# Suffix sums of a stick-breaking attention taken over added key blocks, and the cached keys and values loaded later

## The chip, the core and the metric

The kernel runs on one core of a Trainium2 chip. The metric is the device time of one execution in microseconds; the time before is the median of three runs, 817.32 us (816.03 to 822.58). TensorE is called PE here, its weight loads PEld, VectorE is DVE, ScalarE is ACT, GpSimd is POOL, and SP is the queue that starts most loads.

## What is computed

One layer of a hybrid trunk over 544 tokens (512 of a new stream, 32 of a running one with 256 cached frames). The part that matters here is the attention of the 512 new tokens:

```python
z = einsum('bqhd,bkhd->bhqk', q, k) * DH ** -0.5
causal = k_pos[None, :] < q_pos[:, None]
log_not = where(causal, log_sigmoid(-z), 0.0)
suffix = cumsum(log_not, axis=3, reverse=True) - log_not
a = where(causal, exp(log_sigmoid(z) + suffix), 0.0)
o = einsum('bhqk,bkhd->bqhd', a, v)
```

So the score of key s for query t gets the sum of `-softplus(z)` over the keys from s to t-1: its own and all later ones before the query. Around it stand the input projection (queries, keys, values, a pooling input, gates), a pooling branch, output projections, an MLP of 4 x 1024 hidden features, a gated input embedding and norms. The running stream attends to its 256 cached frames and its own 32.

## The kernel before, in words

Everything lies features first: a tile has 128 features as partitions and tokens as columns. Matrix products are in fp32r, and each factor is split into a high part (ACT copies it to fp32r) and a low part (DVE subtracts), so that a product is three matmuls: hi x hi, hi x lo, lo x hi. A weight tile is 128x1024; SP loads it into `raw`, `split(t)` on ACT makes `w_hi` (L635) and `split(t)` on DVE `w_lo` (L1324), up to three tiles ahead of PE. A projection tile (`tile`, L984, L987, L990) is 48 matmuls of 272 columns.

The mixer stage is a loop over four pairs of heads (`pair(i)` on PE, ACT and DVE; the first and last are written out, the middle two are a hardware loop). The order of each engine's work is written out by hand, one queue per engine. On PE a pair is: tile 0, tile 1, `sums(1, i-1)`, tile 2, `outputs(1, i-1)`, `scores(0, i)`, tile 3, `v_rows`, tile 4, tile 5, `sums(0, i)`, tile 6, `outputs(0, i)`, `scores(1, i)`, tile 7. Tiles 0 to 3 give q, k, v and the pooling input, 4 to 7 the gates. A projection result has two places in PSUM in turn: tile j may start once DVE has taken tile j-2. `gate(3, i)` (L1422) takes tile 7, so tile 1 of the next pair waits for it.

The attention of a head, g = 2i + hh, runs through these steps. Keys are partitions, in four blocks b of 128; the columns of block b are the queries of the blocks b to 3, 512, 384, 256 and 128 of them, 1280 columns in all, held in one PSUM region `z_ps` and one SBUF buffer `work` at the offsets `Z_OFF`:

- `scores` (PE) writes z; `chain` (ACT, L703, L705, L707) makes log(1 + exp(-|z|)); `stick` (DVE, L1401) adds max(z, 0): the sticks, softplus(z).
- POOL zeroes the non-causal corners of the four diagonal blocks with four selects of 128x128 (`mask_diagonals`, L584).
- `stick_hi` (ACT, L712) and `stick_lo` (DVE, L1406) split the sticks into `b_hi` and `b_lo`; the second signals `slo_done`.
- `sums` (PE, L1037) waits for `slo_done` and adds to z. For key block b and each block c from b to 3 it multiplies the sticks of block c by a constant matrix: `negtri` (a triangle of -1) for c = b, `negone` (all -1) for c > b, each for the high and the low part.
- `prob` (ACT, L718) takes exp; POOL masks again; `prob_hi` (L723) and `prob_lo` (L1411) split; `outputs` (PE, L965 to L967) multiplies by the values; `head_out` (L1417) takes the result.

In a middle pair DVE does `stick(1)`, `stick_lo(1)`, `gate(3)` at the end. In the last pair the order is `stick(1)`, `gate(3)`, `mean_lo(2)` (L1428, L1429), `group_lo(0)` (L1434), `mean_lo(3)`, `group_lo(1)`, `stick_lo(1)`, while PE does after tile 7 `group(0)` to `group(3)` (the pooling groups, six matmuls of 272 columns each, by way of L965 to L967), then `sums(1, 3)`, four `pool_part`s, `outputs(1, 3)` and then the scores against the cached keys (L1143), before which it waits for `past_in`: both loads of cached keys (`ckt`) and values (`cvn`), 512 KB each. ACT issues these loads (L786, L787) after the first pair.

Of the kernel before, what the change touches and what calls it, by code (L numbers as in the profile page):

```python
# [12 lines left out]
P = 128  # L13
# [213 lines left out]
def hybrid_step_kernel(nc, w_tiles, x_t, p_t, ck_t, cv, state_t, w_grp, vecs,  # L227
                       y_t, k_t, v_t, pool_t):
    ctx = ExitStack()
    with ctx:  # L230
# [3 lines left out]
        def sem(name):  # L234
            return ctx.enter_context(nc.semaphore(name))
# [23 lines left out]
        def at(part, name, shape, dt=F32):  # L259
            t = nc.alloc_sbuf_tensor_at(name, shape, dt, offset=place[part])  # L260
            place[part] += 4 * int(np.prod(shape[1:]))
            return t
# [3 lines left out]
        gates = at(0, "gates", [P, 2 * KT, TOK])  # L266
        upad = at(1, "upad", [P, GROUPS, PADW])
        ysb = at(1, "ysb", [P, PAIRS, TOK])
        ckt = at(1, "ckt", [P, PAIRS, PAST])
        cvn = at(1, "cvn", [P, PAST // P, HEADS * DH])  # L270
        mean0 = [at(1, "mean0_hi", [P, TOK], F32R), at(1, "mean0_lo", [P, TOK], F32R)]
        qbd = at(1, "qbd", [P, PAIRS, 2 * DEC])
# [131 lines left out]
        spm_done = sem("spm_done")  # L404
        shi_done = sem("shi_done")
        slo_done = sem("slo_done")
        c_done = sem("c_done")
        prob_done = sem("prob_done")
        pm_done = sem("pm_done")
# [213 lines left out]
        def _(act):  # L623
# [85 lines left out]
            def stick_hi(hh, i):  # L709
                g = 2 * i + hh  # L710
                act.wait_ge(spm_done, g * QB + QB)
                act.activation(b_hi[:, SOF:SOF + Z_COLS], work[:, :], ACT.Copy).then_inc(shi_done, 1)  # L712

            def prob(hh, i):
                g = 2 * i + hh

                act.wait_ge(c_done, g + 1)
                act.activation(work[:, :], z_ps, ACT.Exp).then_inc(prob_done, 1)  # L718

            def prob_hi(hh, i):  # L720
                g = 2 * i + hh
                act.wait_ge(pm_done, g * QB + QB)
                act.activation(b_hi[:, SOF:SOF + Z_COLS], work[:, :], ACT.Copy).then_inc(phi_done, 1)  # L723
# [59 lines left out]
                stick_hi(1, i)  # L783

            pair(0)
            act.dma_start(ckt[:, :, :], ck_t).then_inc(past_in, 16)  # L786
            act.dma_start(cvn[:, :, :], cv).then_inc(past_in, 16)  # L787
            with act.Fori(1, PAIRS - 1) as i:
                pair(i)
            pair(PAIRS - 1)  # L790
# [2 lines left out]
            split(T_MIX + AHEAD)  # L793
            split(T_MIX + 1 + AHEAD)
            prob(1, PAIRS - 1)
            prob_hi(1, PAIRS - 1)
            split(T_MIX + 2 + AHEAD)

# [163 lines left out]
        def _(pe):  # L962
# [65 lines left out]
            def sums(hh, i):  # L1028

                g = 2 * i + hh  # L1030
                pe.wait_ge(slo_done, g + 1)
                for b in range(QB):
                    for c in range(b, QB):
                        lhs = negtri if c == b else negone
                        z = z_ps[:, Z_OFF[b] + P * (c - b):Z_OFF[b] + Z_LEN[b]]
                        for part in (b_hi, b_lo):
                            mm = pe.matmul(z, lhs[:, :], part[:, SOF + Z_OFF[c]:SOF + Z_OFF[c] + Z_LEN[c]],  # L1037
                                           start=False, stop=(c == QB - 1), skip_group_check=True)
                mm.then_inc(c_done, 1)

            def outputs(hh, i):
# [269 lines left out]
        def _(dve):  # L1311
# [8 lines left out]
            def split(t, i=0, per=0):  # L1320

                s = t % W_RING
                dve.wait_ge(whi_done, t + 1 + i * per)
                dve.tensor_tensor(w_lo[:, s, :, :].rearrange("p k c -> p (k c)"), raw[:, t % RAW_RING, :],  # L1324
                                  w_hi[:, s, :, :].rearrange("p k c -> p (k c)"), ALU.subtract).then_inc(wlo_done, 1)
# [71 lines left out]
            def stick(hh, i):  # L1397
# [3 lines left out]
                dve.scalar_tensor_tensor(out=work[:, :], in0=z_ps, scalar=0.0, in1=work[:, :],  # L1401
                                         op0=ALU.max, op1=ALU.add).then_inc(sp_done, 1)

            def stick_lo(hh, i):
                dve.wait_ge(shi_done, 2 * i + hh + 1)
                dve.tensor_tensor(b_lo[:, SOF:SOF + Z_COLS], work[:, :], b_hi[:, SOF:SOF + Z_COLS],  # L1406
                                  ALU.subtract).then_inc(slo_done, 1)

            def prob_lo(hh, i):
                dve.wait_ge(phi_done, 2 * i + hh + 1)  # L1410
# [8 lines left out]
            def gate(jj, i):  # L1419
                j = 4 + jj  # L1420
                dve.wait_ge(full, j + 1 + i * S1_PER)
                dve.tensor_tensor(halves(gates[:, 4 * i + jj, :]), pair_result(j, i), halves(rn[:, :]), ALU.mult)\  # L1422
                   .then_inc(taken, 1)
# [14 lines left out]
            def pair(i):  # L1438
                first = isinstance(i, int) and i == 0
                last = isinstance(i, int) and i == PAIRS - 1  # L1440
                q, k, v = (ev[:, n, 0:TOK] for n in range(3))
                if not first:
                    split(AHEAD + 0, i, S1_PER)

                dve.wait_ge(full, 1 + i * S1_PER)
                dve.scalar_tensor_tensor(out=halves(q), in0=pair_result(0, i), scalar=DH ** -0.5, in1=halves(rn[:, :]),
                                         op0=ALU.mult, op1=ALU.mult).then_inc(taken, 1)
                dve.wait_ge(taken, 1 + i * S1_PER)
                for h in range(2):
                    r = slice(DH * h, DH * (h + 1))  # L1450
                    dve.tensor_copy(qbd[r, i, DEC * h:DEC * (h + 1)], q[r, SEQ:TOK])
                dve.wait_ge(qkhi_done, 2 * i + 1)
                dve.tensor_tensor(b_lo[:, QOF:QOF + TOK], q, b_hi[:, QOF:QOF + TOK], ALU.subtract)\
                   .then_inc(qklo_done, 1)
                split(AHEAD + 1, i, S1_PER)
                if not first:
                    dve.wait_ge(kv_out[0], 16 * i)
                normed(1, k, i, S1_PER, pair_result(1, i)).then_inc(taken, 1)
                dve.wait_ge(taken, 2 + i * S1_PER)
                dve.tensor_copy(kst[:, i, :], k[:, SEQ:TOK])  # L1460
                dve.wait_ge(qkhi_done, 2 * i + 2)
                dve.tensor_tensor(b_lo[:, KOF:KOF + TOK], k, b_hi[:, KOF:KOF + TOK], ALU.subtract)\
                   .then_inc(qklo_done, 1)
                split(AHEAD + 2, i, S1_PER)
                if not first:
                    prob_lo(1, i - 1)
                if not first:
                    dve.wait_ge(kv_out[1], 16 * i)
                normed(2, v, i, S1_PER, pair_result(2, i)).then_inc(taken, 1)
                dve.wait_ge(taken, 3 + i * S1_PER)  # L1470
                dve.tensor_copy(vst[:, i, :], v[:, SEQ:TOK])
                if not first:
                    head_out(1, i - 1)
                    stick(0, i)
                    split(AHEAD + 3, i, S1_PER)

                dve.wait_ge(full, 4 + i * S1_PER)
                u = upad[:, i, :]
                dve.tensor_tensor(u[:, U_PROMPT:U_PROMPT + HALF], pair_result(3, i)[:, 0, :], rn[:, 0:HALF], ALU.mult)
                dve.tensor_tensor(u[:, U_PROMPT + HALF:U_STATE], pair_result(3, i)[:, 1, 0:SEQ - HALF],  # L1480
                                  rn[:, HALF:SEQ], ALU.mult)
                dve.tensor_tensor(u[:, U_SAMPLE:PADW], pair_result(3, i)[:, 1, SEQ - HALF:HALF],
                                  rn[:, SEQ:TOK], ALU.mult).then_inc(taken, 1)
                if first:
                    stick(0, i)
                    split(AHEAD + 3)
                stick_lo(0, i)
                dve.wait_ge(vhi_done, i + 1)
                dve.tensor_tensor(b_lo[:, VOF:VOF + SEQ], o_ps, b_hi[:, VOF:VOF + SEQ], ALU.subtract)\
                   .then_inc(vlo_done, 1)  # L1490
                split(AHEAD + 4, i, S1_PER)
                gate(0, i)
                split(AHEAD + 5, i, S1_PER)
                if last:

                    dve.wait_ge(mean_done, GROUPS)
                gate(1, i)
                split(AHEAD + 6, i, S1_PER)
                if last:
                    mean_lo(0)  # L1500
                    mean_lo(1)
                prob_lo(0, i)
                gate(2, i)
                head_out(0, i)
                split(AHEAD + 7, i, S1_PER)
                stick(1, i)
                if last:
                    gate(3, i)
                    mean_lo(2)
                    group_lo(0)  # L1510
                    mean_lo(3)
                    group_lo(1)
                    stick_lo(1, i)
                    for s in kv_out:
                        dve.wait_ge(s, 16 * PAIRS)
                else:
                    stick_lo(1, i)
                    gate(3, i)

# [320 lines left out]
```

## Time and profile before

| what | value |
|---|---|
| runs, median (lowest to highest) | 817.32 us (816.03 to 822.58) |
| the profiled execution's own time | 817.61 us |
| span of the profiled execution | 815.9 us |
| PE busy | 792.6 us, 97% |
| DVE busy | 473.9 us, 58% |
| ACT busy | 370.4 us, 45% |
| POOL busy | 96.0 us, 12% |
| mean granted TensorE clock | 0.99 |

The span is from the first to the last instruction of the one execution that was profiled, and 1.7 us of its own time lie around it. Times inside the profile are microseconds from the span's start. A row of a timeline is: start, length, engine, line, operation, what it writes and reads, how many, and in brackets how long the engine stood idle before it and what released it. Matmuls overlap in their pipeline, so the pace of PE is read from start to start and not from the lengths.

### The profile page before, as it was taken

To read this page: it belongs to the slowest core of one execution; us is meant where nothing else is said; L and a number is where in the kernel's file an instruction comes from. 1 tells how busy PE (TensorE), PEld (TensorE's weight loads), DVE (VectorE), ACT (ScalarE), POOL (GpSimd) and SP (SyncE) were. 2 spreads that over 40 slices of the span, in tenths; PEclk is the share of its full clock that TensorE was granted. 3 is DMA by queue.
4 is the path that set the end of the run, shared out by engine and by line. 5 is a ranking of instruction groups with operands and counts; after the bars stand their busy time and mean duration, and the time that the engine had idled before them with its cause. 6 is when DMAs were issued, how large, how long until landed. Compare 5 with 4: busy or idle time off the path is not lost.

```text
span 815.9 us, 14392 instructions
## 1 busy us (share of the span) xinstructions
PE 792.6 (97%) x6130; PEld 780.5 (96%) x6130; DVE 473.9 (58%) x555; ACT 370.4 (45%) x423; POOL 96.0 (12%) x164
## 2 busy tenths in 40 slices
PE   8999999999998999999999999999999999999993
PEld 7899999999998989999999999999999999999993
DVE  6654354354455536687873347533773367677966
ACT  7444433433485344466552136422552145555542
POOL 1041041042061000010000200010001100100000
PEclk9999999999999999999999999999999999999997
DMA  6333231231222113967564875667574855925402
GB/s 229 118 98 119 71 94 55 87 92 52 92 69 76 53 53 104 270 181 173 177 207 130 188 199 171 170 176 182 169 197 123 206 184 165 210 72 164 116 1 110
DMA packets 32954, 110.19 MB, mean 135 GB/s; under 512 B 4480, under 2 KB 4480, under 8 KB 32896
## 3 DMA queue, kind: packets, MB, share of 16 engines
q1 hardware_dynamic: 24624, 84.72, 32.0%
q0 software_dynamic: 6016, 21.04, 14.2%
q10 hardware_dynamic: 2256, 3.60, 1.2%
q8 instruction: 45, 0.74, 0.4%
q14 instruction: 13, 0.11, 0.0%
HBM read 94.33 MB, written 4.52 MB: 121 GB/s over the span
## 4 chain that ended last, share of the span: by engine, by line
PE 88%; DVE 7%; ACT 2%; issue 2%; DMA 1%; SPq 0%; DVEq 0%; ACTq 0%
PE psum L1228 23%; PE psum L984 18%; PE psum L990 18%; PE psum L987 18%; PE psum L1037 3%; PE psum L965 2%; PE psum L967 2%; PE psum L966 2%; DVE w_lo L1324 1%; DMA raw<-w_tiles 1%; ACT w_hi L635 1%; DVE work L1348 1%; DVE xt L1750 1%; PE psum L1306 1%; DVE b_lo L1668 0%
## 5 line engine op out<-in xcount | busy, mean ns | idle before, releaser
L643 ACT ACTIVATE w_hi<-raw_more 128x1024 fp32r<-128x1024 f32 x84 | 88.7, 1056 | 136.6 <-PE psum L990 102.6
L984 PE MATMUL psum<-a_hi,w_hi 128*128 128x272 f32 x640 | 135.6, 293 | 2.7 <-DVE a_lo L1338 2.4
L990 PE MATMUL psum<-a_hi,w_lo 128*128 128x272 f32 x640 | 132.8, 289 | 0.0
L987 PE MATMUL psum<-a_lo,w_hi 128*128 128x272 f32 x640 | 132.5, 289 | 0.0
L984 PE MATMUL psum<-b_hi,w_hi 128*128 128x272 f32 x640 | 132.3, 288 | 0.0
L990 PE MATMUL psum<-b_hi,w_lo 128*128 128x272 f32 x640 | 132.2, 288 | 0.0
L987 PE MATMUL psum<-b_lo,w_hi 128*128 128x272 f32 x640 | 132.1, 288 | 0.0
L1332 DVE TENSOR_TENSOR w_lo<-raw_more,w_hi 128x1024 fp32r<-128x1024 f32 x84 | 102.4, 1223 | 36.9 <-ACT w_hi L643 36.6
L1228 PE MATMUL psum<-u_hi,w_hi 128*128 128x272 f32 x560 | 115.9, 288 | 1.1 <-issue 0.9
L1228 PE MATMUL psum<-u_hi,w_lo 128*128 128x272 f32 x560 | 115.7, 288 | 0.0
L1228 PE MATMUL psum<-u_lo,w_hi 128*128 128x272 f32 x560 | 115.5, 287 | 0.0
L984 PEld LDWEIGHTS psum<-a_hi,w_hi 128*128 128x128 f32 x640 | 100.7, 189 | 5.4 <-DVE a_lo L1338 3.4
L987 PEld LDWEIGHTS psum<-a_lo,w_hi 128*128 128x128 f32 x640 | 101.0, 189 | 0.0
L987 PEld LDWEIGHTS psum<-b_lo,w_hi 128*128 128x128 f32 x640 | 100.6, 188 | 0.0
L984 PEld LDWEIGHTS psum<-b_hi,w_hi 128*128 128x128 f32 x640 | 100.5, 188 | 0.0
L990 PEld LDWEIGHTS psum<-a_hi,w_lo 128*128 128x128 f32 x640 | 100.4, 190 | 0.0
L990 PEld LDWEIGHTS psum<-b_hi,w_lo 128*128 128x128 f32 x640 | 100.1, 189 | 0.0
L1228 PEld LDWEIGHTS psum<-u_hi,w_hi 128*128 128x128 f32 x560 | 87.8, 188 | 1.6 <-issue 1.4
L1228 PEld LDWEIGHTS psum<-u_lo,w_hi 128*128 128x128 f32 x560 | 88.4, 188 | 0.0
L1228 PEld LDWEIGHTS psum<-u_hi,w_lo 128*128 128x128 f32 x560 | 87.5, 188 | 0.0
L1324 DVE TENSOR_TENSOR w_lo<-raw,w_hi 128x1024 fp32r<-128x1024 f32 x42 | 52.7, 1255 | 58.9 <-ACT w_hi L635 58.9
L1582 DVE TENSOR_TENSOR xt<-psum,xt 128x544 f32<-128x544 f32 x40 | 28.9, 723 | 89.3 <-PE psum L990 89.3
(192 smaller groups left out, 987.4 us busy)
## 6 DMA issues: line engine op xcount, KB each, us to landing
raw_more<-w_tiles SPq DMA_DIRECT2D x84, 512.0 KB, 4.3
raw<-w_tiles SPq DMA_DIRECT2D x67, 512.0 KB, 3.5
raw_more<-w_tiles POOLq DMA_DIRECT2D x16, 512.0 KB, 7.2
raw_more<-raw_more POOLq DMA_DIRECT2D x14, 512.0 KB, 8.4
xt<-x_t SPq DMA_DIRECT2D x8, 272.0 KB, 5.1
y_t<-xt SPq DMA_DIRECT2D x8, 272.0 KB, 2.1
raw<-w_tiles POOLq DMA_DIRECT2D x4, 512.0 KB, 7.9
raw_more<-raw POOLq DMA_DIRECT2D x3, 512.0 KB, 6.4
```

Of the source, the lines that this page charges most:

```text
L643: act.activation(w_hi[:, t % W_RING, :, :].rearrange("p k c -> p (k c)"), src, ACT.Copy)\
L965: pe.matmul(out, hi, rhi, start=first, stop=False, skip_group_check=True)
L966: pe.matmul(out, hi, rlo, start=False, stop=False, skip_group_check=True)
L967: return pe.matmul(out, lo, rhi, start=False, stop=last, skip_group_check=True)
L984: pe.matmul(base[:, h, :], w_hi[:, s, wk, :], cols(hi, k, h * HALF, (h + 1) * HALF), start=(opens and q == 0), stop=False, skip_group_chec ...
L987: pe.matmul(base[:, h, :], w_hi[:, s, wk, :], cols(lo, k, h * HALF, (h + 1) * HALF), start=False, stop=False, skip_group_check=True)
L990: mm = pe.matmul(base[:, h, :], w_lo[:, s, wk, :], cols(hi, k, h * HALF, (h + 1) * HALF), start=False, stop=(closes and q == len(ks) - 1), ...
L1037: mm = pe.matmul(z, lhs[:, :], part[:, SOF + Z_OFF[c]:SOF + Z_OFF[c] + Z_LEN[c]], start=False, stop=(c == QB - 1), skip_group_check=True)
L1228: mm = pe.matmul(out[:, two, :], w_part[:, t % W_RING, 2 * k + two, :], u_part[:, op, k, :], start=(OPENS[s] and k == 0 and w_part is w_hi ...
L1324: dve.tensor_tensor(w_lo[:, s, :, :].rearrange("p k c -> p (k c)"), raw[:, t % RAW_RING, :], w_hi[:, s, :, :].rearrange("p k c -> p (k c)" ...
L1332: dve.tensor_tensor(w_lo[:, t % W_RING, :, :].rearrange("p k c -> p (k c)"), src, w_hi[:, t % W_RING, :, :].rearrange("p k c -> p (k c)"), ...
L1582: dve.tensor_tensor(halves(xt[:, m, :]), slot(n), halves(xt[:, m, :]), ALU.add).then_inc(taken, 1)
```

## The change

A second way of taking the sums of later key blocks. DVE adds up the sticks of the later blocks first, three blocks of 128 columns, into `later`; ACT and DVE split `later` into `later_hi` and `later_lo` (384 columns each). `sums` then has for each key block its own sticks against `negtri`, the next block's first 128 columns against `negone`, and for the blocks 0 and 1 the added sticks against `negone` for the rest. The new buffers lie in the place of `ckt` and `cvn`, so the loads of these move behind the last `prob`. `stick_later` stands behind `split(AHEAD + 3)` for the first head of a pair, and behind `stick(1)` for the second, in the last pair behind `gate(3)`.

```diff
@@ buffers
+        later_hi = nc.alloc_sbuf_tensor_at("later_hi", [P, 3 * P], F32R, offset=place[1])
+        later_lo = nc.alloc_sbuf_tensor_at("later_lo", [P, 3 * P], F32R, offset=place[1] + 3 * P * 4)
         ckt = at(1, "ckt", [P, PAIRS, PAST])
+        later = nc.alloc_sbuf_tensor_at("later", [P, 3 * P], F32, offset=place[1])
         cvn = at(1, "cvn", [P, PAST // P, HEADS * DH])
@@ ACT, stick_hi
                 act.activation(b_hi[:, SOF:SOF + Z_COLS], work[:, :], ACT.Copy).then_inc(shi_done, 1)
+                act.wait_ge(later_done, g + 1)
+                act.activation(later_hi[:, :], later[:, :], ACT.Copy).then_inc(laterhi_done, 1)
@@ ACT, the order
             pair(0)
-            act.dma_start(ckt[:, :, :], ck_t).then_inc(past_in, 16)
-            act.dma_start(cvn[:, :, :], cv).then_inc(past_in, 16)
             with act.Fori(1, PAIRS - 1) as i:
...
             prob(1, PAIRS - 1)
+            act.dma_start(ckt[:, :, :], ck_t).then_inc(past_in, 16)
+            act.dma_start(cvn[:, :, :], cv).then_inc(past_in, 16)
             prob_hi(1, PAIRS - 1)
@@ PE, sums
+                sticks = [(b_hi[:, SOF:SOF + Z_COLS], later_hi), (b_lo[:, SOF:SOF + Z_COLS], later_lo)]
                 for b in range(QB):
-                    for c in range(b, QB):
-                        lhs = negtri if c == b else negone
-                        z = z_ps[:, Z_OFF[b] + P * (c - b):Z_OFF[b] + Z_LEN[b]]
-                        for part in (b_hi, b_lo):
-                            mm = pe.matmul(z, lhs[:, :], part[:, SOF + Z_OFF[c]:SOF + Z_OFF[c] + Z_LEN[c]],
-                                           start=False, stop=(c == QB - 1), skip_group_check=True)
+                    at_b = Z_OFF[b]
+                    for own, _ in sticks:
+                        mm = pe.matmul(z_ps[:, at_b:at_b + Z_LEN[b]], negtri[:, :], own[:, at_b:at_b + Z_LEN[b]],
+                                       start=False, stop=(b == QB - 1), skip_group_check=True)
+                    if b == QB - 1:
+                        continue
+                    nxt = Z_OFF[b + 1]
+                    for own, _ in sticks:
+                        mm = pe.matmul(z_ps[:, at_b + P:at_b + 2 * P], negone[:, :], own[:, nxt:nxt + P],
+                                       start=False, stop=(b == QB - 2), skip_group_check=True)
+                    if b < QB - 2:
+                        more = (slice(0, 2 * P), slice(2 * P, 3 * P))[b]
+                        for _, sums_of in sticks:
+                            mm = pe.matmul(z_ps[:, at_b + 2 * P:at_b + Z_LEN[b]], negone[:, :], sums_of[:, more],
+                                           start=False, stop=True, skip_group_check=True)
@@ DVE
+            def stick_later(hh, i):
+                g = 2 * i + hh
+                one, two, three = (work[:, Z_OFF[b]:Z_OFF[b] + Z_LEN[b]] for b in (1, 2, 3))
+                dve.wait_ge(spm_done, g * QB + QB)
+                dve.tensor_tensor(later[:, 2 * P:3 * P], two[:, P:2 * P], three, ALU.add).then_inc(later_part, 1)
+                dve.tensor_tensor(later[:, 0:P], one[:, P:2 * P], two[:, 0:P], ALU.add)
+                dve.wait_ge(later_part, g + 1)
+                dve.tensor_tensor(later[:, P:2 * P], one[:, 2 * P:3 * P], later[:, 2 * P:3 * P], ALU.add)\
+                   .then_inc(later_done, 1)
             def stick_lo(hh, i):
                 dve.wait_ge(shi_done, 2 * i + hh + 1)
-                dve.tensor_tensor(b_lo[:, SOF:SOF + Z_COLS], work[:, :], b_hi[:, SOF:SOF + Z_COLS],
-                                  ALU.subtract).then_inc(slo_done, 1)
+                dve.tensor_tensor(b_lo[:, SOF:SOF + Z_COLS], work[:, :], b_hi[:, SOF:SOF + Z_COLS], ALU.subtract)
+                dve.wait_ge(laterhi_done, 2 * i + hh + 1)
+                dve.tensor_tensor(later_lo[:, :], later[:, :], later_hi[:, :], ALU.subtract).then_inc(slo_done, 1)
@@ DVE, pair
                     split(AHEAD + 3, i, S1_PER)
+                    stick_later(0, i)
...
                 if first:
                     stick(0, i)
                     split(AHEAD + 3)
+                    stick_later(0, i)
                 stick_lo(0, i)
...
                 stick(1, i)
                 if last:
                     gate(3, i)
+                    stick_later(1, i)
                     mean_lo(2)
...
                 else:
+                    stick_later(1, i)
                     stick_lo(1, i)
                     gate(3, i)
```

## Rows read from the trace of the kernel before

**Rows 1.** The page's fourth part: lines on the chain that ended last.

```profile
PE psum L1228 23%; PE psum L984 18%; PE psum L990 18%; PE psum L987 18%; PE psum L1037 3%; PE psum L965 2%; PE psum L967 2%; PE psum L966 2%; DVE w_lo L1324 1%; DMA raw<-w_tiles 1%; ACT w_hi L635 1%; DVE work L1348 1%; DVE xt L1750 1%; PE psum L1306 1%; DVE b_lo L1668 0%
```

**Rows 2.** Busy time by stretch, L1037 alone: stretch, PE, PEld, clock, DMA, GB/s.

```profile
115.20:117.90 2.70, 2.70 (x20) 2.60 (x20) 1.00 0.11 42
...
266.30:269.60 3.30, 3.26 (x20) 3.10 (x20) 0.85 0.02 5
```

**Rows 3.** Timeline of PE, one call of `sums`.

```profile
146.36 0.40 PE L1037 MATMUL psum<-b_hi,negtri 128*128 128x512 f32 x1
...
147.41 0.22 PE L1037 MATMUL psum<-b_hi,negone 128*128 128x128 f32 x1
147.47 0.27 PE L1037 MATMUL psum<-b_lo,negone 128*128 128x128 f32 x1
147.58 0.39 PE L1037 MATMUL psum<-b_hi,negtri 128*128 128x384 f32 x1
147.81 0.34 PE L1037 MATMUL psum<-b_lo,negtri 128*128 128x384 f32 x1
147.98 0.28 PE L1037 MATMUL psum<-b_hi,negone 128*128 128x256 f32 x1
...
148.84 0.28 PE L1037 MATMUL psum<-b_hi,negtri 128*128 128x128 f32 x1
...
149.07 0.46 PE L984 MATMUL psum<-a_hi,w_hi 128*128 128x272 f32 x2
```

**Rows 4.** Timelines of DVE, PE and PEld where pair 2's tile 1 begins.

```profile
137.99 1.49 DVE L1406 TENSOR_TENSOR b_lo<-work,b_hi 128x1280 fp32r<-128x1280 f32 x1 [2.44 <-ACT b_hi L712]
139.40 0.72 DVE L1422 TENSOR_TENSOR gates<-psum,rn 128x544 f32 x1
...
139.86 0.41 PE L990 MATMUL psum<-a_hi,w_lo 128*128 128x272 f32 x2
...
140.23 0.30 PEld L984 LDWEIGHTS psum<-a_hi,w_hi 128*128 128x128 f32 x2 [0.18 <-issue]
```

**Rows 5.** Timeline of DVE, the copies of tile 3 in pair 2.

```profile
165.67 0.43 DVE L1479 TENSOR_TENSOR upad<-psum,rn 128x272 f32 x1
166.02 0.40 DVE L1480 TENSOR_TENSOR upad<-psum,rn 128x240 f32 x1
```

**Rows 6.** Timeline of DVE, head 0; then L1037's starts, first to last.

```profile
47.50 2.47 DVE L1406 TENSOR_TENSOR b_lo<-work,b_hi 128x1280 fp32r<-128x1280 f32 x1 [2.24 <-ACT b_hi L712]
...
L1037 PE MATMUL psum<-b_hi,negtri x32: 275/359/796, 52.7 to 269.4; 128*128 128x512 f32 x8, 128*128 128x384 f32 x8, 128*128 128x256 f32 x8, 128*128 128x128 f32 x8
```

**Rows 7.** Timelines of DVE and POOL at the last pair's end; POOL also in pair 1.

```profile
261.69 0.68 DVE L1428 TENSOR_TENSOR b_lo<-upad,b_hi 128x512 fp32r<-128x512 f32 x1
...
263.88 0.77 DVE L1434 SCALAR_TENSOR_TENSOR a_lo<-psum,vec,a_hi 128x544 fp32r<-128x544 f32 x1
264.79 1.49 DVE L1406 TENSOR_TENSOR b_lo<-work,b_hi 128x1280 fp32r<-128x1280 f32 x1
...
261.70 0.82 POOL L584 TENSOR_SCALAR_AFFINE_SELECT work<-work 128x128 f32<-128x128 f32 x1
...
261.21 0.54 POOL L584 TENSOR_SCALAR_AFFINE_SELECT work<-work 128x128 f32<-128x128 f32 x2 [15.70 <-DVE work L1401]
...
135.63 1.02 POOL L584 TENSOR_SCALAR_AFFINE_SELECT work<-work 128x128 f32<-128x128 f32 x4 [10.87 <-DVE work L1401]
```

**Rows 8.** Busy by stretch: PE, PEld, DVE, ACT, POOL, then clock, DMA, GB/s.

```profile
260.50:263.90 3.40, 1.71 (x11) 1.38 (x11) 3.40 (x8) 1.73 (x3) 1.56 (x4) 1.00 0.49 154
263.90:267.30 3.40, 3.29 (x12) 2.62 (x11) 3.02 (x5) 2.28 (x4) 0.00 (x0) 0.50 0.00 0
```

**Rows 9.** The load of the cached values; the last `prob`; the first use.

```profile
cvn<-cv ACTq DMA_DIRECT2D x1, 512.0 KB, 4.4
...
276.87 1.22 ACT L718 ACTIVATE work<-psum 128x1280 f32<-128x1280 f32 x1
...
284.03 1.95 PE L1143 MATMUL psum<-qbd,ckt 128*128 128x64 f32 x16
```

More of the change, by code:

```diff
@@ L406, in hybrid_step_kernel @@
         slo_done = sem("slo_done")
+        later_part = sem("later_part")
+        later_done = sem("later_done")
+        laterhi_done = sem("laterhi_done")
         c_done = sem("c_done")
```

## The prediction, made before the changed kernel ran

> **What bounds the kernel now.** I read the page first: PE is busy 97% of the span, the chain that ended last is PE nearly from end to end, and L1037, the suffix sums, is 3% of it [rows 1]. So PE's time in these sums counts, and any new wait of PE costs in full. Next the view of busy time by stretch for L1037 alone: one head takes 2.7 us with the full clock, and 3.3 us for the last head, where the mean granted clock was 0.85 [rows 2]. The timeline of PE then gives the pace from start to start inside one head: 20 matmuls from 146.36 to 149.07, which is 2.71 us [rows 3]. Last I looked for places where PE already leans on DVE, since the change gives DVE more to do. There are two such places: a gap of some 0.15 us at tile 1 of the pairs 1, 2 and 3 [rows 4], and the end of the last pair, where PE goes from one DVE result to the next and the clock falls [rows 8].
>
> **What is removed from PE.** Per head the column count falls from 5120 to 4096 and the matmuls from 20 to 18. Matched piece by piece, two matmuls of 384 columns go, two of 256 become 128 wide, all others stay. A 384-column one paces at 0.17 us (147.81 to 147.98). A 128-column one takes 0.06 us right behind a wider one, but the next needs 0.11 us (147.41, 147.47, 147.58), and a pair behind other 128-column ones takes 0.23 us (148.84 to 149.07), so they pace at some 0.115 us each, no faster than the 256-column ones (about 0.12 us) [rows 3]. Gain per head: 2 x 0.17 and next to nothing for the narrowing, 0.355 us with rounding; 18 matmuls in some 2.36 us. Bounds: 2 of 20 matmuls at the mean pace, 0.27 us, taken down to 0.25; and with the narrowing paid in full (2 x 0.06), 0.46. I take 0.355, for the trace shows 128-column pairs at both paces and the new order has more of the slow kind. Eight heads: -2.84 us.
>
> The Trainium skill, TensorE: Matmul & The Clock Gate, "Wait — 56ns, not 53.3ns?", says that warm matmuls follow each other at N columns / 2.4 GHz plus about 2.5 ns. By that rule a head would gain 0.43 us and eight heads 3.45 us, 0.6 more than my sum. The rows on the 128-column pairs disagree with it here, and I go by them.
>
> **What DVE and ACT get.** No row shows an addition of 128 columns, so I take it from its neighbours: 272 columns last 0.43 us and let the next start after 0.35 [rows 5]; 512 last 0.68 [rows 7]; hence 1.04 ns a column, and pace is length less 0.08. An addition of 128: 0.28 us long, paced 0.20. The subtraction of 384: 0.55 long, paced 0.47. `stick_later` is then 0.6 us of DVE, `later_lo` 0.47, and the 384-column copy about 0.5 on ACT. Bounds for `later_lo`: the 272-column row, 0.35, and the 512-column one, 0.6.
>
> *Before the sums of heads 0 to 6.* `stick_lo` of head 0 ends at 49.97 and its sums start at 52.7 [rows 6]; this is the tightest of the seven, the others have six or seven us (139.48 to 146.36 for head 3 [rows 3, 4]). `later_lo` adds 0.5 to 1 us (`stick_lo` itself stretches from 1.49 to 2.47 beside POOL's window sums). Hidden; bounds 0 and 0.
>
> *Tile 1 of the pairs 1, 2 and 3.* Here it isn't hidden. PE's last pair of tile 0 starts at 139.86, so the next would follow at 140.11; the weights of tile 1 are loaded at 140.23. That is 0.11 us after `gate(3)` ended (139.40 + 0.72), and tile 1 needs the place that this op frees. The profile books the 0.18 us as "issue", but the same gap and distance stand at pairs 1 and 3. Before `gate(3)` stands `stick_lo`, and it starts when ACT has copied the masked sticks: a chain that began with the scores of the second head [rows 4]. `stick_later` fits beside that copy: DVE had idled 2.44 us before `stick_lo`, of which the 1.28 us behind the masks are free. `later_lo` doesn't fit, for it stands between `stick_lo` and `gate(3)`: +0.47 us, three times, +1.41 us (bounds 3 x 0.35 and 3 x 0.6; nothing, if the gap has another cause). Queued behind `gate(3)` are only `split` and the next q, which PE doesn't miss.
>
> *The last pair.* DVE goes `gate(3)`, `mean_lo(2)` at 261.69, and so on to `group_lo(1)` at 263.88 and `stick_lo` at 264.79, which ends at 266.28; PE starts the last sums then, at 266.3 [rows 2, 7]. Now `stick_later` stands before `mean_lo(2)` and waits for POOL's four masks, with all of that queued behind it and PE's `group(2)`, `group(3)` and sums waiting. The masks began at 261.21. The third lasted 0.82 us beside `mean_lo(2)`; undisturbed, four take 1.02 (135.63) [rows 7]. With DVE waiting they end at 262.24, `stick_later` starts at 262.3, and with 0.6 us and a hop `mean_lo(2)` starts at 262.95: +1.26. `stick_lo` had waited 0.14 us for ACT behind `group_lo(1)` (263.88 + 0.77 to 264.79); that slack goes, so it starts 1.1 later, and `later_lo` adds 0.47 behind it: the sums start 1.53 us later. Bounds: 1.1 (shorter additions, no hop) and 2.0 (masks at 1.56 us as before).
>
> The Trainium skill, SBUF — State Buffer, "SBUF: two separate sides", says that a DVE op with two SBUF inputs and a GpSimd op that reads SBUF lock each other out for a whole instruction. The third mask beside `mean_lo(2)` agrees. With the masks as long as before, against this rule, the sum would be 0.5 us higher.
>
> *The clock.* In 260.50 to 263.90 PE was busy for 1.71 of 3.4 us, and in the 3.4 us after that the clock was 0.50 (1.2 GHz) [rows 8]; this cost the last sums 0.6 us [rows 2]. PE's gaps get longer here. For the sum I take the same 0.6 again, so no difference; bounds -0.6 and +1.7 (one further stretch of 3.4 us at half pace on the path).
>
> *Cached keys and values.* `prob` starts at 276.87, both loads are issued while it runs, by 277.6, and PE needs them at 284.03. The values took 4.4 us to land [rows 9]: 282.0, two us early. Price 0; if SP's weight tile beside it doubled the landing, +2.4. ACT waits for POOL's masks then, so the issue is hidden.
>
> **Sum.** -2.84 + 1.41 + 1.53 = +0.10 us. The profiled execution took 817.61 us itself (span 815.9 and 1.7 around it), which gives 817.7. It lies 0.3 above the median of the runs, so I forecast 817.4 us for the median.
>
> **Rivals.**
> - *The gain comes whole.* The gap at tile 1 is PE's own ("issue", as the profile books it), and DVE's additions in the tail cost nothing because PE would idle at half clock anyway. For it: the booking. Against: PE waits on named DVE results in the tail. 817.3 - 2.84 = 814.5; with tile 1 alone free, 816.0.
> - *A second cold stretch, the slower side.* PE's gaps before the last sums grow by 1.5 us in all, and behind the gaps of 260.5 to 263.9 the clock fell [rows 8]. If the gaps before `group(2)`, `group(3)` and the sums bring a second fall behind the first, the sums and the `pool_part`s behind them run at 1.2 GHz for a further 3.4 us, half of it lost: +1.7, 819.1. It decides from the point where PE stands as idle after 264 as it did before. For it: the gaps double. Against: at half pace the two groups fill more of the time, and the sums come right behind.
> - *The narrow matmuls give less*, 0.25 us a head: +0.84, 818.2.
> - *The loads land late*: PE stands before L1143, 2.4 us at a doubled landing, 819.8. Against: two us of cover.
>
> **How the numbers follow.** Cancelled out, 817.4: 0.50. Gain whole or half: 0.17. Second cold stretch: 0.18. Narrow matmuls give less: 0.10. Late loads: 0.05. The range has the bounds of the terms in it: the low end 814.8 nearly reaches the whole gain, the high end 820.6 is the sum with `later_lo` at 0.6 (+0.4), a tail of 2.0 (+0.5), the cold stretch (+1.7) and a part of what the narrow matmuls may give less. A measurement of this kernel can tell about 1%, 8 us, from no change, and every case lies inside: within 1% 0.95, faster 0.02, slower 0.03 (one run of before was 822.58, so disturbances of that size exist).
>
> **What would show it.** Right: a head's sums from start to start in 2.35 us with 18 matmuls; the gap before tile 1 at 0.6 us where it was 0.15, behind a later `gate(3)`; `stick_lo` in the last pair later by 1.1 us and the last sums by 1.5 against tile 7; no wait before L1143. Wrong: tile 1 following without a larger gap, the clock low for more than one stretch near 264, or a wait on `past_in`.

## The result, and the profile after

Twelve runs of the changed kernel have a median of 820.82 us (817.64 to 823.29), against 817.57 us (815.99 to 822.58) of the kernel before in the same series. The ratio is 1.0031, with a 95% interval of 1.0016 to 1.0046: slower by 0.3%, clear of noise and well within 1%. The forecast was 817.4 us and no change; the ratio times the 817.32 us that it started from is 819.9, inside the range, while the median itself lies 0.2 us above the range's end. The profiled execution took 817.75 us (span 816.0), 0.14 more than the one of before, where +0.10 was forecast. So the profile has about what was worked out, and the mean of many executions turns out (below) some 2 us longer than that. The rest is about both halves.

The page's first part of the changed kernel:

```profile
PE 790.5 (97%) x6114; PEld 778.6 (95%) x6114; DVE 483.8 (59%) x587; ACT 373.6 (46%) x431; POOL 93.4 (11%) x164
```

PE has 2.1 us less to do, DVE 9.9 us more. One head's sums in the timeline of PE, changed kernel (it answers to [rows 3]):

```profile
145.21 0.40 PE L1046 MATMUL psum<-b_hi,negtri 128*128 128x512 f32 x1
...
145.68 0.22 PE L1053 MATMUL psum<-b_hi,negone 128*128 128x128 f32 x1
145.74 0.27 PE L1053 MATMUL psum<-b_lo,negone 128*128 128x128 f32 x1
145.85 0.33 PE L1058 MATMUL psum<-later_hi,negone 128*128 128x256 f32 x1
...
146.67 0.28 PE L1058 MATMUL psum<-later_hi,negone 128*128 128x128 f32 x1
146.78 0.28 PE L1058 MATMUL psum<-later_lo,negone 128*128 128x128 f32 x1
146.89 0.33 PE L1046 MATMUL psum<-b_hi,negtri 128*128 128x256 f32 x1
...
147.57 0.47 PE L994 MATMUL psum<-a_hi,w_hi 128*128 128x272 f32 x2
```

145.21 to 147.57 is 2.36 us where it was 2.71, and so for the first seven heads: 0.35 us gained each. The last head went from 3.24 to 2.47 us, for in this execution the clock was back at 2.4 GHz when its sums began. The two paces of a 128-column matmul are seen again, 0.06 us behind a wider one and 0.11 in a row.

Where pair 2's tile 1 begins, timelines of DVE and PE (to [rows 4]):

```profile
136.39 1.49 DVE L1437 TENSOR_TENSOR b_lo<-work,b_hi 128x1280 fp32r<-128x1280 f32 x1 [0.61 <-ACT b_hi L720]
137.80 0.55 DVE L1439 TENSOR_TENSOR later_lo<-later,later_hi 128x384 fp32r<-128x384 f32 x1
138.27 0.72 DVE L1454 TENSOR_TENSOR gates<-psum,rn 128x544 f32 x1
...
138.26 0.41 PE L1000 MATMUL psum<-a_hi,w_lo 128*128 128x272 f32 x2
139.13 0.49 PE L994 MATMUL psum<-a_hi,w_hi 128*128 128x272 f32 x2 [0.46 <-DVE gates L1454]
```

`later_lo` takes 0.47 us of DVE's queue, `gate(3)` starts that much later, and what the profile had booked as "issue" is now a wait on it by name. PE goes from 138.26 to 139.13 where 0.25 would do: 0.62 us, against 0.15 before.

The end of the last pair, timelines of DVE, POOL and PE (to [rows 7]):

```profile
259.05 0.71 DVE L1454 TENSOR_TENSOR gates<-psum,rn 128x544 f32<-128x544 f32 x1
260.26 0.29 DVE L1429 TENSOR_TENSOR later<-work 128x128 f32<-128x128 f32 x1 [0.50 <-POOL work L592]
...
260.88 0.69 DVE L1460 TENSOR_TENSOR b_lo<-upad,b_hi 128x512 fp32r<-128x512 f32 x1
...
263.67 1.48 DVE L1437 TENSOR_TENSOR b_lo<-work,b_hi 128x1280 fp32r<-128x1280 f32 x1
265.07 0.55 DVE L1439 TENSOR_TENSOR later_lo<-later,later_hi 128x384 fp32r<-128x384 f32 x1
...
259.20 1.02 POOL L592 TENSOR_SCALAR_AFFINE_SELECT work<-work 128x128 f32<-128x128 f32 x4 [15.71 <-DVE work L1422]
...
259.82 0.39 PE L975 MATMUL psum<-b_hi 128*128 128x272 f32 x1 [1.22 <-DVE gates L1454]
262.42 0.60 PE L975 MATMUL psum<-b_hi 128*128 128x272 f32 x1 [1.58 <-DVE a_lo L1466]
265.68 0.50 PE L1046 MATMUL psum<-b_hi,negtri 128*128 128x512 f32 x1
```

The four masks took 1.02 us while DVE ran `gate(3)`, which takes its large input from PSUM, and then stood still for 0.50 us. From `gate(3)` to `mean_lo(2)` it is 1.83 us (259.05 to 260.88) where it was 0.63, and PE has a second wait, 1.58 us before `group(2)`, that was 0.47.

Last, busy time by stretch (PE, PEld, DVE, ACT, POOL, clock, DMA, GB/s; to [rows 8]), changed kernel:

```profile
258.40:261.80 3.40, 1.22 (x8) 0.80 (x6) 2.90 (x8) 1.63 (x3) 1.02 (x4) 1.00 0.50 154
262.00:265.40 3.40, 2.98 (x12) 2.80 (x12) 3.40 (x6) 1.88 (x3) 0.00 (x0) 0.50 0.00 0
299.50:302.90 3.40, 3.40 (x24) 3.00 (x24) 0.58 (x2) 0.06 (x1) 0.00 (x0) 1.00 0.00 0
302.90:306.30 3.40, 3.40 (x17) 3.40 (x16) 1.02 (x2) 3.40 (x7) 0.00 (x0) 0.51 0.02 5
```

PE is busy for 1.22 us ahead of the fall where it was 1.71. There is also a stretch at 1.2 GHz at 303 us, in projections that never wait, behind the small matmuls of the running stream. The profile of before has the same small matmuls and no such stretch there, but one at 38.6 us, behind PE's wait of 1.6 us before the first scores; the changed kernel waits there just as long (1.58 us), and its clock stayed up. So, apart from the last ten microseconds of both, there are two such stretches each, in different places, and each is 3.4 us long. That sets the question: does the change make them more frequent over many executions, or has the series found a wait that the profile doesn't show?

### The profile page after: what moved, and what is told of

The parts are those of the page before. It is cut to its first block, busy times and chain, and to the rows that moved or that the text cites. A ratio compares the mean times of both kernels' runs of the same rounds, so it can differ in the third digit from the quotient of the medians.

```text
span 816.0 us, 14404 instructions
## 1 busy us (share of the span) xinstructions
PE 790.5 (97%) x6114; PEld 778.6 (95%) x6114; DVE 483.8 (59%) x587; ACT 373.6 (46%) x431; POOL 93.4 (11%) x164
## 4 chain that ended last, share of the span: by engine, by line
PE 80%; issue 7%; DVE 7%; ACT 4%; POOL 1%; DMA 0%; DVEq 0%; SPq 0%; ACTq 0%; POOLq 0%
PE psum L1249 23%; PE psum L994 16%; PE psum L1000 16%; PE psum L997 16%; PE psum L975 2%; PE psum L977 2%; PE psum L976 2%; PE psum L1046 1%; DVE w_lo L1345 1%; ACT w_hi L643 1%; POOL work L592 1%; DVE work L1422 1%; ACT work L713 1%; ACT work L711 1%; DVE xt L1786 1%
```

## The experiments

Every kernel below ran in series with the kernel before. Of the kernel before, 89 runs in three of these series (c0 to e3, e4 to e7, e8 to e10) have a mean of 818.1 us at a mean granted clock of 0.9909. The means of the single series lie between 818.1 and 818.3, so kernels of different series can be compared by their means. "Mean" below is over the kernel's runs; the clock is the mean of what each run granted over its span.

**The changed kernel again.** No edit.

> The changed kernel once more, unchanged. Theory A (the pace of the path is as forecast, +0.1 us, and the rest of the measured loss is stretches at 1.2 GHz, each worth about 1.7 us, that come more often with the changed kernel): over its runs, time falls on a straight line against the mean granted clock, about 4 us for each 0.01 of clock; its runs lie 2 to 3 us over those of the kernel before and at a lower mean clock by 0.003 to 0.004. Theory B (a wait that the one profile did not show, paid at full clock in most runs): the same 2 to 3 us, but at a mean clock equal to that of the kernel before.

Median 819.41 us (816.52 to 823.43, 12 runs), ratio 1.0022 (1.0003 to 1.0041). With the first series that is 24 runs, mean 820.1 us at a clock of 0.9884: 2.0 us and 0.0025 of clock from the kernel before. Over these 24 the time falls by 7.1 us for each 0.01 of clock, and 0.25 of that is 1.8 us, nearly the whole distance: theory A in kind. Its sizes were off: the 12 runs alone lie 1.6 us over the kernel before at a clock 0.0020 lower, where 2 to 3 us and 0.003 to 0.004 were expected, and the slope isn't 4 but 7.1. The slope fits the profiles: 3.4 us at half clock lower the mean over 816 us by 0.0021, and with PE busy throughout they cost 1.7 us, some 8 us for 0.01 (an estimate). The profile of c0 is of one of its longer executions, 821.94 us; busy time by stretch:

```profile
259.70:263.10 3.40, 1.35 (x9) 0.91 (x7) 2.90 (x8) 1.50 (x3) 1.02 (x4) 1.00 0.50 154
263.20:266.50 3.30, 2.66 (x11) 2.66 (x12) 3.30 (x6) 2.11 (x3) 0.00 (x0) 0.50 0.00 0
266.60:269.90 3.30, 3.16 (x12) 2.65 (x12) 3.13 (x4) 1.66 (x2) 0.00 (x0) 0.50 0.00 0
...
304.10:307.40 3.30, 3.30 (x15) 3.06 (x15) 1.52 (x4) 1.31 (x3) 0.00 (x0) 0.51 0.00 0
307.50:310.80 3.30, 3.30 (x17) 3.30 (x16) 0.00 (x0) 3.30 (x7) 0.00 (x0) 0.50 0.02 5
```

Same program, and PE's waits before the groups are the same (1.22 and 1.56 us), but both places now stay at 1.2 GHz twice as long, and a fifth stretch of 3.4 us lies at 14 us. Here is the "second cold stretch" of the rivals, with the last sums in it: they took 3.78 us (267.10 to 270.88).

**The loads alone.**

```diff
             pair(0)
-            act.dma_start(ckt[:, :, :], ck_t).then_inc(past_in, 16)
-            act.dma_start(cvn[:, :, :], cv).then_inc(past_in, 16)
...
             prob(1, PAIRS - 1)
+            act.dma_start(ckt[:, :, :], ck_t).then_inc(past_in, 16)
+            act.dma_start(cvn[:, :, :], cv).then_inc(past_in, 16)
```

> The kernel before with only the loads of cached keys and values moved behind the last prob. Theory A: no difference, within 1 us of the kernel before, both loads landed before PE needs them at some 284 us, 2 us of cover. Rival (the moved loads are the cost, in runs where they land late): 1.5 to 3 us slower than before, with PE waiting before L1143.

817.78 us, ratio 1.0001 (0.9985 to 1.0017), mean 818.0. The moved loads cost nothing. In the changed kernel's timeline of ACT they are issued even before `prob` runs, for ACT's queue has passed `prob` on while the weight copy still works:

```profile
274.47 1.06 ACT L643 ACTIVATE w_hi<-raw 128x1024 fp32r<-128x1024 f32 x1 [7.23 <-PE psum L1000]
274.52 0.35 ACTq L804 DMA_DIRECT2D ckt<-ck_t  x1
274.90 0.46 ACTq L805 DMA_DIRECT2D cvn<-cv  x1
275.44 1.22 ACT L728 ACTIVATE work<-psum 128x1280 f32<-128x1280 f32 x1
```

The values landed 4.4 us later, at 279.3; PE's first matmul on the keys started at 282.60, without a wait.

The profile of e1 is of its longest execution, 821.13 us, and it shows something else. PE and DVE do at the last pair's end what they do in the kernel before, with waits of 1.22, 0.46 and 0.30 us ahead of the groups, and the clock still stayed down twice as long. Busy time by stretch:

```profile
264.50:267.90 3.40, 3.10 (x10) 2.48 (x10) 3.02 (x4) 2.29 (x4) 0.00 (x0) 0.50 0.00 0
267.90:271.30 3.40, 3.40 (x16) 3.40 (x16) 1.62 (x2) 0.52 (x1) 0.00 (x0) 0.51 0.12 25
```

A stretch at 1.2 GHz lies at 305 us too. So neither the long fall near 264 nor the one near 303 belongs to the change alone; what the change can do is make them more frequent. Of its 24 executions 10 have a clock of 0.987 or less, of 106 of the kernel before 13.

**The matmuls alone.** This kernel leaves the sums over later blocks out: the matmuls for them read plain sticks.

```diff
-                act.wait_ge(later_done, g + 1)
-                act.activation(later_hi[:, :], later[:, :], ACT.Copy).then_inc(laterhi_done, 1)
...
-                sticks = [(b_hi[:, SOF:SOF + Z_COLS], later_hi), (b_lo[:, SOF:SOF + Z_COLS], later_lo)]
+                sticks = [(b_hi[:, SOF:SOF + Z_COLS], b_hi[:, SOF:SOF + Z_COLS]), (b_lo[:, SOF:SOF + Z_COLS], b_lo[:, SOF:SOF + Z_COLS])]
...
-                dve.wait_ge(laterhi_done, 2 * i + hh + 1)
-                dve.tensor_tensor(later_lo[:, :], later[:, :], later_hi[:, :], ALU.subtract).then_inc(slo_done, 1)
```

and `stick_later` with its four calls is gone.

> The changed kernel without the additions, the copy to later_hi and the subtraction to later_lo; the matmuls keep their shapes and read other sticks in their place, so the sums of later blocks are left out. Theory A: the 18 matmuls give 0.35 us a head, no new waits: 2.8 us faster than before (span 813.1 for equal stretches at 1.2 GHz), gap before tile 1 back at 0.15 us. Rival (the narrow matmuls give less, 0.25 us a head): 2.0 us faster. If the matmuls themselves lower the clock: no gain or a loss.

814.88 us, ratio 0.9956 (0.9938 to 0.9973), mean 814.75 at 0.9920: 3.4 us faster (the interval reaches from some 2 to 5 us). Some 0.8 us of it goes with the clock, which is 0.0011 higher, at 7.1 us for 0.01; what is left is near the 2.84 of eight heads. The matmuls by themselves don't lower the clock. The gap before tile 1 is 0.15 us again.

**The added work alone**: the changed kernel with the loop of 20 matmuls of before in `sums`. `later_hi` and `later_lo` are made and not read.

> The changed kernel with the 20 matmuls of before: the additions and the two splits are made and not used. Theory A: 0.47 us at three tile 1 boundaries and 1.1 to 1.5 us in the last pair, +2.5 to +2.9 us, and stretches at 1.2 GHz on top as in the changed kernel, so 4 to 6 us slower than before. Rival (the loss lies in the matmuls or the loads): +2.5 to +2.9 us only.

822.63 us, ratio 1.0062 (1.0042 to 1.0082), 6 runs, mean 822.9 at 0.9882: 4.8 us slower. The waits account for 1.4 + 1.35 = 2.75 of it, the clock for most of the rest. In its profile the last sums lay wholly at 1.2 GHz:

```profile
264.60:268.00 3.40, 1.46 (x9) 1.13 (x9) 3.40 (x9) 2.95 (x4) 0.00 (x0) 1.00 0.02 6
268.10:274.80 6.70, 6.18 (x26) 5.67 (x25) 3.90 (x5) 1.66 (x2) 0.00 (x0) 0.51 0.19 72
```

The two halves, -3.4 and +4.8, add up to +1.4 us; 2.0 was measured for the whole. So the expected gain is there, and it is given back by the added work on DVE and ACT, partly as waits and partly as clock.

**`gate(3)` first.**

```diff
                 else:
+                    gate(3, i)
                     stick_later(1, i)
                     stick_lo(1, i)
-                    gate(3, i)
```

> The changed kernel with gate(3) ahead of stick_later(1) and stick_lo(1) in the pairs 0 to 2. Theory A (later_lo delays gate(3), for which tile 1 waits): the gap of 0.61 us before tile 1 goes altogether, three times, 1.8 us faster than the changed kernel, while gate(3) lies beside POOL's masks. Rival (tile 1 waits for something else): gap and time unchanged.

818.81 us (816.30 to 820.16), mean 818.5: 1.6 us faster than the changed kernel (give or take 1.2 by the spread of the runs, as for the next two comparisons), where 1.8 was expected, although the clock is lower, 0.987 against 0.9884. The gap is gone. Timelines of DVE and PE in pair 2:

```profile
137.38 1.49 DVE L1437 TENSOR_TENSOR b_lo<-work,b_hi 128x1280 fp32r<-128x1280 f32 x1 [0.61 <-ACT b_hi L720]
138.79 0.55 DVE L1439 TENSOR_TENSOR later_lo<-later,later_hi 128x384 fp32r<-128x384 f32 x1
139.26 1.22 DVE L1345 TENSOR_TENSOR w_lo<-raw,w_hi 128x1024 fp32r<-128x1024 f32 x1
...
139.24 0.42 PE L1000 MATMUL psum<-a_hi,w_lo 128*128 128x272 f32 x2
139.49 0.41 PE L994 MATMUL psum<-a_hi,w_hi 128*128 128x272 f32 x2
139.74 0.41 PE L997 MATMUL psum<-a_lo,w_hi 128*128 128x272 f32 x2
```

PE keeps its 0.25 us per two matmuls across the boundary; DVE does `gate(3)` in the time in which it waits for the masks. The 0.15 us gap of the kernel before goes too, so it was a wait on `gate(3)`.

**The last pair's `stick_later` behind `group_lo(1)`.**

```diff
                 if last:
                     gate(3, i)
-                    stick_later(1, i)
                     mean_lo(2)
                     group_lo(0)
                     mean_lo(3)
                     group_lo(1)
+                    stick_later(1, i)
                     stick_lo(1, i)
```

> The changed kernel with stick_later(1) of the last pair behind group_lo(1) in place of ahead of mean_lo(2). Theory A: PE's wait before group(2) falls from 1.58 to 0.47 us, the last sums start some 0.3 us sooner, and stretches at 1.2 GHz near 262 get rarer: the mean clock rises by 0.001 to 0.002, and the kernel is 1 to 2 us faster than the changed one. Rival (only the delay of the last sums counts): 0.3 us faster, clock unchanged.

819.38 us, mean 818.8 at 0.990: 1.3 us faster than the changed kernel, the clock up by 0.0016. In its profile PE's wait before `group(2)` is 0.46 us, as expected, and there is no stretch at 1.2 GHz near 264; PE waits 1.45 us ahead of the last sums instead, which start 6.13 us after `gate(3)` where it was 6.63. Both moves together:

> Both reorderings. Theory A: 3 to 4 us faster than the changed kernel, 1 to 1.5 us faster than the kernel before (sum of -2.84, nothing at tile 1 and the 0.15 us gaps gone too, +1.0 in the last pair). Rival (the loss lies elsewhere): still slower than the kernel before.

816.95 us (814.23 to 820.68), ratio to the kernel before 0.9995 (0.9980 to 1.0011), mean 817.2 at 0.9898. 2.9 us faster than the changed kernel, as the parts add up, but at the low edge of the 3 to 4 us expected, and not told from the kernel before, over which 1 to 1.5 us were expected: the clean path is shorter, but the runs still spread over 6 us.

**PE kept busy in the two waits.** If waits and clock are the matter, useless work in the wait should make the kernel faster.

```diff
+            pe.wait_ge(y_done, HEADS - 1)
             for g in range(GROUPS):
+                for _ in range((0, 9, 11, 0)[g]):
+                    pe.matmul(psum[:, 7, 0:HALF], negone[:, :], cols(a_hi, 0, 0, HALF), start=True, stop=True,
+                              skip_group_check=True)
                 group(g)
```

> The changed kernel with 9 matmuls of 272 columns ahead of group(1) and 11 ahead of group(2), results unused, in the time in which PE waits there (1.2 and 1.6 us); a wait for head 6's result goes ahead of the groups, which has long been met. Theory A (part of the loss is the clock falling behind these waits): no stretch at 1.2 GHz begins between 255 and 270 us, mean clock up by 0.002 or more, 1.5 to 2.5 us faster than the changed kernel although PE has more to do. Rival (the clock isn't lowered by these waits): same clock, same time or some tenths slower.

817.78 us, and above all 817.19 to 819.30 in twelve runs where the changed kernel has 816.5 to 823.4. Mean 818.0 at 0.9925: 2.1 us faster than the changed kernel (give or take 1.0) with 20 matmuls more. The longest executions have gone. Its profile has no stretch at 1.2 GHz between 255 and 270 us, as expected; the one at 303 us is still there. Busy time by stretch in this kernel:

```profile
259.00:262.00 3.00, 2.92 (x23) 2.69 (x22) 2.50 (x6) 1.24 (x2) 1.02 (x4) 1.00 0.54 175
262.00:265.40 3.40, 2.84 (x19) 2.21 (x17) 3.40 (x7) 2.48 (x4) 0.00 (x0) 1.00 0.00 0
```

**The control**: the same in the kernel before, with `(0, 9, 3, 0)`, since its second wait is short.

> The kernel before with unused matmuls only in the last pair's waits: 9 ahead of group(1), 3 ahead of group(2). It is the control for e7, where filling the same place took 2.1 us off the changed kernel's mean time. Theory A (the change makes the clock's falls in that place more frequent and longer): the kernel before gains less, 0.5 to 1.2 us, with its clock up by 0.001. Rival (both kernels lose the same there, and the measured loss of the change is something else): 2 us gained here too.

818.73 us, ratio 1.0000 (0.9986 to 1.0014), mean 818.4 against 818.3 of its series, the clock 0.9916. It gains nothing, less even than I expected; by the spread of the runs a gain of 1 us can just be excluded, the 2 us of the rival clearly. So the same filling takes 2.1 us off the changed kernel and nothing measurable off the kernel before: the change makes the falls of the clock in this place cost more. That it does so by the second wait, 1.58 us in place of 0.47, is what e5 points to (with that wait short again the clock rose by 0.0016), but 1.3 us give or take 1.2 don't prove it, and e1's profile shows the long fall with a short second wait. The profile of e11 has no fall near 264, but one of 6.8 us near 38: one execution doesn't tell what the mean does.

**Everything together, in both kernels.** `gate(3)` first, the waits before the groups filled, and 11 more matmuls (on PSUM bank 4, behind a wait for `taken` at 3) ahead of the first scores, where PE stands for 1.6 us; e10 has the last `stick_later` moved besides, and its unused matmuls spread as the waits then lie (9, 3 and 2 ahead of the groups 1 to 3, 9 ahead of the last sums).

> The changed kernel with gate(3) first in the pairs 0 to 2, the 9 and 11 unused matmuls ahead of group(1) and group(2), and 11 more ahead of the first scores, where PE waits 1.6 us. Theory A: no stretch at 1.2 GHz left near 38 or 262 us, mean clock 0.994 or more, all runs within 2 us of each other; time from the clean path: 820.1 less 1.8 (gate) less 2.1 (fill) less some 1 (early stretch), 815 us. Rival: no better than e4, 818.5.

> The kernel before with the same treatment: gate(3) ahead of stick_lo(1) in the pairs 0 to 2, unused matmuls in PE's waits (11 ahead of the first scores, 9 ahead of group(1), 3 ahead of group(2)). Theory A: the three gaps of 0.15 us go (0.45 us), the stretches at 1.2 GHz near 38 and 264 go, 816 us, 2 us under the kernel before. Rival (the kernel before loses nothing to such stretches): 817.6.

> As e8, with stick_later(1) of the last pair behind group_lo(1) and the unused matmuls spread to its waits (9, 3 and 2 ahead of the groups 1 to 3, 9 ahead of the last sums). Theory A: 0.5 us under e8, 814.5 us, and 1.5 to 2 us under e9: with equal clocks the change is worth 2.84 less what it delays in the last pair (1.0). Rival (the change is worth nothing even so): e9 and e10 equal.

| kernel | median (lowest to highest) | ratio to before (95%) | mean | clock |
|---|---|---|---|---|
| e8, changed, gate and fill | 815.07 (814.51 to 818.05) | 0.9969 (0.9956 to 0.9983) | 815.6 | 0.9936 |
| e9, before, gate and fill | 815.86 (815.55 to 817.43) | 0.9978 (0.9965 to 0.9990) | 816.3 | 0.9938 |
| e10, changed, all | 815.63 (814.10 to 816.42), 8 runs | 0.9973 (0.9962 to 0.9983) | 815.4 | 0.9935 |

All three beat both kernels, by 0.2 to 0.3%. At nearly equal clocks the change is worth 0.7 to 0.9 us by the means, give or take 0.8, and 0.8 and 0.2 us by the medians; by the intervals of their ratios e8, e9 and e10 are not told apart. Of my 1.5 to 2 us for e10 against e9 about half came, and e10 isn't 0.5 us under e8. For e8 the 815 us came, the clock of 0.994 just about, but the runs spread over 3.5 us and not 2. For e9 the 816 us came: the kernel before, which gained nothing from the filled waits of the last pair alone (e11), gains 2.0 us when the filling before the first scores and `gate(3)` first are added. Three gaps of 0.15 us are 0.45 of that, and the clock, 0.0022 above e11's, goes with most of the rest. The profile of e8 has no stretch at 1.2 GHz between the start and its last ten microseconds (span 813.2).

## Why the prediction was right, and where it wasn't

- *What PE gains.* Forecast 0.355 us a head, measured 0.35 in seven heads (2.71 to 2.36). 128-column matmuls in a row don't pace below 0.11 us here. By the rule in the Trainium skill (TensorE: Matmul & The Clock Gate, "Wait — 56ns, not 53.3ns?") it would have been 0.43 us a head, and the trace disagrees with it.
- *Heads 0 to 6, hidden.* Right for the sums. Head 0 showed a side effect that I hadn't listed: `prob_lo` came late there, and PE waited 0.38 us before the first `outputs`. In that profile the early stretch at 1.2 GHz was missing, so PE was 1.7 us ahead of where it had been.
- *Tile 1.* Forecast +0.47 us three times; measured 0.46 to 0.47 three times (gaps of 0.61, 0.62, 0.62 after 0.16, 0.15, 0.16). Reading "issue" as a wait on `gate(3)` was right, as e4 shows, and without that term the sum would have come out at a gain of 1.3 us.
- *The last pair.* Forecast 1.53 us; from `gate(3)` to the last sums it went from 5.28 (261.06 to 266.34) to 6.63 us (259.05 to 265.68), +1.35. The masks did take 1.02 us instead of 1.56. `mean_lo(2)` came 1.20 us later, where 1.26 was forecast, and `stick_lo` 0.89 (from 3.73 to 4.62 us behind `gate(3)`), where 1.1 was: the short second part of `mean_lo(2)` (L1429 before, L1461 after), no longer beside the masks, let the next operation start after 0.10 us in place of 0.20, and the slack ahead of `stick_lo` was 0.2 us and not 0.14. The Trainium skill (SBUF — State Buffer, "SBUF: two separate sides") says that a DVE op with two SBUF inputs and a GpSimd op that reads SBUF lock each other out; the masks' 1.02 us without such an op beside them agree.
- *The loads.* Cost 0, shown by e1.
- *The sum* of these, -2.8 + 1.4 + 1.35, is -0.1 us by what was measured, +0.10 as forecast, and the two profiled executions differ by 0.14. That the two agree so well is partly luck: PE's wait at head 0 (0.38 us) and the last head's larger gain (0.77 us in place of 0.35) were in no sum and cancel, and so do the stretch at 38.6 us that only the one execution had and the one at 303 us that only the other had, 1.7 us each.
- *The clock* is the step that was mis-sized. I wrote "For the sum I take the same 0.6 again, so no difference", and gave one further stretch a chance of 0.18. Measured, the mean clock went from 0.9909 to 0.9884, and at 7.1 us for 0.01 that is 1.8 us of the 2.0 us between the means. With the waits before `group(1)` and `group(2)` filled, 2.1 us go and the clock rises to 0.9925 (e7); the same in the kernel before brings nothing measurable (e11). So the change adds falls of the clock behind these waits in part of the executions, as c0's profile shows one. The slower rival (a second cold stretch, +1.7) was thus, in the mean of many executions, about the case that came. The mistake was to price the clock by one profile: such stretches come and go between executions of one program, and the term should have been an expected value over them, at least half of the rival's price.

What stays open: how the clock's falls are spread over the three places (38, 262 and 303 us) in each kernel, since one profile per kernel shows one execution; and whether what precedes 303 us, where PE doesn't wait, is made more frequent by the change. It isn't peculiar to it: the profiles of e1 and e9, whose matmuls there are those of the kernel before, have a stretch there too. It also isn't shown which of the two waits before the groups does the harm. e6 against e7 isn't settled either: their times differ by less than the spread.

## What to carry to other kernels

Taking matmuls from the bounding engine pays only what isn't handed to a queue that this engine already leans on; look for such places by tiny gaps with a fixed length, whatever the profile books them under, and price each instruction put before the op that ends them. When a change lengthens a wait of TensorE next to another one, expect that the clock may answer, and judge by many executions with their granted clocks: two profiled executions that agree to 0.2 us said nothing about 2 us here. Where a wait can't be avoided, unused matmuls in it can be cheaper than the wait alone, but not everywhere: the last pair of the kernel before gained nothing from them.

## What the runs showed that I had not expected

- Useless work made the kernel faster and steadier: 20 matmuls more, 2.1 us less, and a spread of 2.1 us in place of 6.9.
- A fall of the clock needs no wait of PE: at 303 us of the changed kernel it comes behind 3.4 us in which PE is busy by the record throughout, with mostly small matmuls (24 in 3.4 us). It needn't come either: behind the same small matmuls (23 in the 3.4 us up to 303.5) the clock of the kernel before stayed at 1.00.
- ACT's queue issued the loads 0.9 us before the activation that stands ahead of them in the program had started, its semaphore having long been reached.
